# Attention keys moved between partitions by SP's transfers in place of ScalarE copies, in a two-layer hybrid decoder

## What is computed

```python
aq = apply_partial_rope(aq.reshape(B, S, nh, ATT_HEAD_DIM), cos, sin)
ak = apply_partial_rope(ak.reshape(B, S, nh, ATT_HEAD_DIM), cos, sin)
for gi, (window, dilation) in enumerate(ATT_GROUPS):      # (128, 1), (512, 4), (2048, 16)
    o, lse = dilated_window_attention(aq[:, :, hs], ak[:, :, hs], av[:, :, hs], window, dilation)
```

## Time and profile before

| | |
|---|---|
| runs, median (lowest to highest) | 1271.35 us (1270.79 to 1271.76) |
| profiled execution, span from first to last instruction | 1269.9 us; it has no other time of its own, so what lies around the span is taken as median less span, 1.45 us |
| granted TensorE clock, mean | 0.997 of full |
| PE busy | 1257.0 us, 99% |
| DVE / ACT / POOL busy | 893.0 (70%) / 705.4 (56%) / 244.0 us (19%) |
| bytes moved by DMA | 264.97 MB, mean 209 GB/s |

### The profile page before, as it was taken

One profiled execution on the slowest core, in us unless ns is written; L12 is line 12 of the kernel. 1 busy time (PEld: TensorE's weight loads), 2 busy tenths in 40 slices (PEclk: granted clock), 3 DMA queues, 4 the chain that ended last, 5 costly groups with the idle time before them and its releaser, 6 DMA issues.

```text
span 1269.9 us, 16388 instructions
## 1 busy us (share of the span) xinstructions
PE 1257.0 (99%) x6342; PEld 1040.2 (82%) x6342; DVE 893.0 (70%) x1229; ACT 705.4 (56%) x989; POOL 244.0 (19%) x268
## 2 busy tenths in 40 slices
PE   9999999999999999999999999999999999999996
PEld 8888888878888888888888788888888888888885
DVE  5686876876667655865785779768665776567656
ACT  5477476575555544444563775666755555345441
POOL 0321522522220000400003223334131200004000
PEclk9999999999999999999999999999999999999998
DMA  9968768765665555465657587678546556565562
GB/s 336 310 209 261 236 189 277 260 192 164 204 195 174 184 186 185 152 230 190 207 186 238 183 282 245 193 258 282 184 149 215 183 157 209 165 197 198 186 212 86
DMA packets 129277, 264.97 MB, mean 209 GB/s; under 512 B 8824, under 2 KB 8976, under 8 KB 128688
## 3 DMA queue, kind: packets, MB, share of 16 engines
q1 hardware_dynamic: 123712, 247.23, 60.6%
q0 software_dynamic: 3680, 13.28, 3.0%
q10 hardware_dynamic: 1808, 3.42, 0.7%
HBM read 258.61 MB, written 5.28 MB: 208 GB/s over the span
## 4 chain that ended last, share of the span: by engine, by line
PE 86%; ACT 4%; DVE 4%; POOL 3%; issue 2%; DVEq 0%; POOLq 0%; ACTq 0%
PE ps L373 79%; ACT arena L810 2%; DVE w_lo L1060 2%; ACT w_hi L736 2%; PE ps L444 1%; PE ps L671 1%; PE ps L391 1%; PE ps L639 1%; POOL arena L1684 1%; PE ps L533 0%; POOL arena L1680 0%; PE ps L518 0%; ACT arena L807 0%; PE ps L355 0%; DVE arena L1133 0%
## 5 line engine op out<-in xcount | busy, mean ns | idle before, releaser
L1060 DVE TENSOR_TENSOR w_lo<-w_raw,w_hi 128x1024 fp32r<-128x1024 f32 x408 | 527.1, 1305 | 326.4 <-ACT w_hi L736 324.5
L736 ACT ACTIVATE w_hi<-w_raw 128x1024 fp32r<-128x1024 f32 x408 | 427.3, 1058 | 388.9 <-PE ps L373 339.3
L373 PE MATMUL ps<-w_hi,xT_hi 128*128 128x512 f32 x1616 | 636.2, 394 | 0.7 <-DVE w_lo L1060 0.7
L373 PE MATMUL ps<-w_hi,xT_lo 128*128 128x512 f32 x1616 | 629.6, 390 | 0.0
L373 PE MATMUL ps<-w_lo,xT_hi 128*128 128x512 f32 x1616 | 629.0, 389 | 0.0
L373 PEld LDWEIGHTS ps<-w_hi,xT_hi 128*128 128x128 f32 x1616 | 303.4, 188 | 64.3 <-issue 1.3
L373 PEld LDWEIGHTS ps<-w_hi,xT_lo 128*128 128x128 f32 x1616 | 303.3, 188 | 64.0
L373 PEld LDWEIGHTS ps<-w_lo,xT_hi 128*128 128x128 f32 x1616 | 303.6, 188 | 61.4
L292 POOL TENSOR_TENSOR carried<-ident 1x1 f32<-1x1 f32 x30 | 19.6, 652 | 454.8 <-DVE arena L1416 178.7
L1217 DVE CUSTOM_DVE_ANT_0 mix<-xres,mix 128x1024 f32<-128x1024 f32 x64 | 89.0, 1390 | 1.1
L807 ACT ACTIVATE arena<-arena 32x256 f32<-32x256 f32 x128 | 53.2, 416 | 15.6 <-DVE arena L1137 14.0
(11 more groups left out here) (244 smaller groups left out, 825.3 us busy)
## 6 DMA issues: line engine op xcount, KB each, us to landing
w_raw<-w_in_dram SPq DMA_DIRECT2D x367, 512.0 KB, 4.5
w_raw<-w_out_dram SPq DMA_DIRECT2D x64, 512.0 KB, 4.8
mix<-gate_w_dram SPq DMA_DIRECT2D x32, 512.0 KB, 5.6
xres<-x_dram ACTq DMA_DIRECT2D x4, 512.0 KB, 8.4
v_dram<-arena POOLq DMA_DIRECT2D x4, 512.0 KB, 6.3
z<-v_dram POOLq DMA_DIRECT2D x8, 256.0 KB, 5.6
z<-ln_g_dram POOLq DMA_DIRECT2D x2, 1024.0 KB, 7.7
store<-ln_b_dram POOLq DMA_DIRECT2D x2, 1024.0 KB, 7.9
```

The costliest lines, as they stand in the source:

```text
L373: mm = pe.matmul(ps[2 * s + t][:], a[:, order[c] * KC + k, t * P:(t + 1) * P], b[:, k], start=(c + k + i == 0), stop=(c == CH - 1 and k == ...
L736: A(hi_of(n, c), w_raw[:, c % RING], ACT.Copy).then_inc(w_hi_done, 1)
L1060: TTn(lo_of(n, c), w_raw[:, c % RING], hi_of(n, c).bitcast(F32), ALU.subtract).then_inc(w_lo_done, 1)
```

## The change

Keys no longer go through ACT. After `turned`, SP issues sixteen transfers within SBUF (32 partitions x 256 elements, 32 KB each) from `zT[1]` to `kT`, in its queue after the load of piece 3 of block `n0+3` and behind a wait for the turn. A transfer keeps the order of elements in a partition (in comp groups two runs of 128 elements a partition, in group 2 one of 256), so `kT` now holds its columns in the order (u, t, m, ...) and PE reads them in runs of 8 elements (comp groups) or 32 (group 2). For that the key turn of group 2 writes its output in four strips. PE waits for `qT_act` (from ACT) and for 256 counts of `kT_landed`. ACT's `moved` handles queries alone.

```diff
--- before.py
+++ after.py
@@ -36,6 +36,7 @@
 ORDER = (1, 2, 0)
 NCOMP = 2
 RES = 4
+QUARTER = P // 4
 LEN = SEQ // RES
 SLOTS = TT * PAIRS
 QUADRANTS = ((0, 0), (1, 0), (0, 1), (1, 1))
@@ -110,13 +111,15 @@
             pass
         arena = sb("arena", [P, 8192])
         qT = arena[:, 0:1024].rearrange("p (m t) -> p m t", m=PAIRS)
-        kT = arena[:, 1024:2048].rearrange("p (m t) -> p m t", m=PAIRS)
+        kT = arena[:, 1024:2048]
         vA = arena[:, 2048:3072].rearrange("p (t c) -> p t c", t=TT)
         pr = arena[:, 3072:4608].rearrange("p (b h s) -> p b h s", b=2, h=2)
         pT_a = arena[:, 4608:5376].rearrange("p (h s) -> p h s", h=2)
         og = arena[:, 5376:6400].rearrange("p (t c) -> p t c", t=TT)
         oacc = arena[:, 6400:7424].rearrange("p (t c) -> p t c", t=TT)
-        qTr, kTr = (m.rearrange("p m (r i) -> p m r i", r=RES) for m in (qT, kT))
+        qTr = qT.rearrange("p m (r i) -> p m r i", r=RES)
+        kTr = kT.rearrange("p (u t m r i) -> p m r t u i", u=4, t=TT, m=PAIRS, r=RES)
+        kTt = kT.rearrange("p (u t m s) -> p m t u s", u=4, t=TT, m=PAIRS)
         vS = vA.rearrange("p t (h q d) -> p t q h d", h=2, q=PAIRS)
         prC = arena[:, 3072:4096].rearrange("p (s h i) -> p s h i", s=SLOTS, h=2)
         zp = arena[:, 0:1024]
@@ -216,7 +219,7 @@
         consts, tables = sem("consts"), sem("tables")
         own_dve, own_pool, own_act = sem("own_dve"), sem("own_pool"), sem("own_act")
         mask_set, roped, turned = sem("mask_set"), sem("roped"), sem("turned")
-        qk_ps, qkT_act, qkT_dve = sem("qk_ps"), sem("qkT_act"), sem("qkT_dve")
+        qT_act, kT_landed = sem("qT_act"), sem("kT_landed")
         scored, masked, probs = sem("scored"), sem("masked"), sem("probs")
         pT_ps, pT_act, pT_dve = sem("pT_ps"), sem("pT_act"), sem("pT_dve")
         pv_done, og_act, og_dve = sem("pv_done"), sem("og_act"), sem("og_dve")
@@ -298,6 +301,20 @@
         @block.sync
         def _(sp):
             for l in range(DEPTH):
+                def move_keys(g):
+
+                    sp.wait_ge(turned, l * (GROUPS * 2) + g * 2 + 2)
+                    for u in range(4):
+                        for f in range(4):
+                            dst = kT[f * QUARTER:(f + 1) * QUARTER, u * 256:(u + 1) * 256]
+                            src = zT[1][u * QUARTER:(u + 1) * QUARTER]
+                            if g < NCOMP:
+                                dst = dst.rearrange("p (t x) -> p t x", t=TT)
+                                src = src.rearrange("p (t f x) -> p f t x", t=TT, f=4)[:, f]
+                            else:
+                                src = src[:, f * 256:(f + 1) * 256]
+                            sp.dma_start(dst, src).then_inc(kT_landed, 16)
+
                 def load(w, n, col, order, gate=()):
 
                     for c in range(CH):
@@ -325,6 +342,8 @@
                                      w[l, rows:rows + KC * P, col:col + BW]
                                      .rearrange("(k p) n -> p k n", p=P)
                                      ).then_inc(w_landed[c % RING], 16)
+                        if c == 3 and N_LOOP < n < N_SU and (n - N_LOOP) % 4 == 3:
+                            move_keys((n - N_LOOP) // 4)
 
                 plain = tuple(range(CH))
                 load(w_in, 0, AG * BW, plain)
@@ -497,14 +516,15 @@
                     def scores(p):
 
                         if p == 0:
-                            pe.wait_ge(qkT_act, qk + 2)
+                            pe.wait_ge(qT_act, l * GROUPS + g + 1)
+                            pe.wait_ge(kT_landed, (l * GROUPS + g + 1) * 16 * 16)
                             pe.wait_ge(comp_og_act, comp)
                             pe.wait_ge(comp_og_dve, comp)
                         for h in range(2):
                             rows = slice(HD * h, HD * (h + 1))
                             o = ps[4 + 2 * (p % 2) + h]
-                            pe.matmul(o[:, 0:P], qT[rows, p, 0:P], kT[rows, p, 0:P], start=True, stop=True)
-                            mm = pe.matmul(o[:, P:3 * P], qT[rows, p, P:2 * P], kT[rows, p, :],
+                            pe.matmul(o[:, 0:P], qT[rows, p, 0:P], kTt[rows, p, 0], start=True, stop=True)
+                            mm = pe.matmul(o[:, P:3 * P], qT[rows, p, P:2 * P], kTt[rows, p],
                                            start=True, stop=True)
                         mm.then_inc(scored, 1)
 
@@ -537,14 +557,15 @@
 
                     def comp_scores():
 
-                        pe.wait_ge(qkT_act, qk + 2)
+                        pe.wait_ge(qT_act, l * GROUPS + g + 1)
+                        pe.wait_ge(kT_landed, (l * GROUPS + g + 1) * 16 * 16)
                         for j in range(TT):
                             for p in range(PAIRS):
                                 at = (j * PAIRS + p) * LEN
                                 for h, c in QUADRANTS:
                                     rows, r = slice(HD * h, HD * (h + 1)), 2 * j + c
                                     mm = pe.matmul(ps[4 + h][c * LEN:(c + 1) * LEN, at:at + LEN], qTr[rows, p, r, :],
-                                                   kTr[rows, p, r, :], start=True, stop=True)
+                                                   kTr[rows, p, r], start=True, stop=True)
                         mm.then_inc(comp_scored, 1)
 
                     def comp_values(comp):
@@ -795,13 +816,13 @@
                             src = src.rearrange("p (q h d) -> p q h d", q=PAIRS, h=2)
                         A(dst, src, ACT.Copy).then_inc(z_act, 1)
 
-                    def moved(which, first, last):
-
-                        act.wait_ge(turned, qk + which + 1)
+                    def moved(first, last):
+
+                        act.wait_ge(turned, qk + 1)
                         for i in range(first, last):
                             u, f = i // 4, i % 4
-                            src = zT[which][u * 32:(u + 1) * 32]
-                            dst = (qT, kT)[which][f * 32:(f + 1) * 32]
+                            src = zT[0][u * 32:(u + 1) * 32]
+                            dst = qT[f * 32:(f + 1) * 32]
                             if g < NCOMP:
 
                                 mv_ = A(dst.rearrange("p m (r t u i) -> p u t (m r) i", r=RES, t=TT, u=4)[:, u],
@@ -810,7 +831,7 @@
                                 mv_ = A(dst.rearrange("p m (t u s) -> p u t m s", t=TT, u=4)[:, u],
                                         src.rearrange("p (t m f s) -> p f t m s", t=TT, m=PAIRS, f=4)[:, f], ACT.Copy)
                         if last == 16:
-                            mv_.then_inc(qkT_act, 1)
+                            mv_.then_inc(qT_act, 1)
 
                     def comp_exponentials():
                         act.wait_ge(comp_masked, comp + 1)
@@ -869,14 +890,10 @@
                     split(n0 + 1, 4, 8)
                     for i in range(4):
                         split(n0 + 2, i, i + 1)
-                        moved(0, 4 * i, 4 * i + 4)
+                        moved(4 * i, 4 * i + 4)
                     take(n0 + 2, 0, z[:, 1, 0, :])
                     split(n0 + 2, 4, 8)
-                    split(n0 + 3, 0, 1)
-                    moved(1, 0, 8)
-                    split(n0 + 3, 1, 2)
-                    moved(1, 8, 16)
-                    split(n0 + 3, 2, 3)
+                    split(n0 + 3, 0, 3)
                     if g < NCOMP:
                         take(n0 + 3, 1, vS[:, 0])
                         split(n0 + 3, 3, 6)
@@ -1130,7 +1147,8 @@
 
                         dve.wait_ge(roped, qk + which + 1)
                         if g == NCOMP:
-                            V.transpose(zT[which], z[:, which].rearrange("p t c -> p (t c)")).then_inc(turned, 1)
+                            into = zT[which].rearrange("p (f b s) -> p b f s", f=4, b=TT * PAIRS) if which else zT[which]
+                            V.transpose(into, z[:, which].rearrange("p t c -> p (t c)")).then_inc(turned, 1)
                             return
                         for t in range(TT):
```

## The result

The kernel with the keys on SP takes 1305.9 us (median of 4 runs, 1304.27 to 1306.46); the kernel before, beside it, 1271.55 (4 runs, 1270.79 to 1272.06). The ratio is 1.0268, with a 95% interval of 1.0253 to 1.0283: **slower by 2.7%**, where the prediction said 1271.7 and at most 1277.5. The profiled execution has a span of 1302.5 us, 32.6 above the 1269.9 of before.

The account below looks back on a forecast made before the run. PE was taken to bound the kernel, a matmul stream without holes. Two group 2 stalls, 0.2 + 0.2 = +0.4 us, on span 1269.9 plus 1.45 to the median gave 1271.7 us; range 1270.6 to 1277.5.

Parts of the forecast that it names:

- What bounds the kernel: PE: busy 1257.0 of 1269.9 us, a matmul stream without holes; waits for ACT's copies only half a microsecond.
- Part 2, the pace: Sixteen key transfers on SP, one issued every 0.45 us, ends 0.38 and 0.64; +0.2 us in each layer's group 2.
- the corner at that end: Start-up pace of 0.64 us on SP: +12.6 us, all four comp groups stalling too; left out of the range.
- the slow landing: Rival: key transfers land after 2.7 us, about +3.0, 1274.4; 1278 with pace 0.54; chance 0.08 of exceeding 2.5 us.
- Part 2, the landing: Key transfers' time from issue to landing: 1.4 us, ends 1.2 and 2.7; keys ready at turn + 8.2 us.
- Part 1: ACT's 96 key copies removed, 39.9 us of ACT: at most -0.5 us; nobody on PE awaits the earlier hi pieces.
- Part 3: Weight loads queued behind SP's sixteen issues: zero, with 0.66 us cover in group 0 of layer 1.
- Part 4: Small ones: transfer traffic, one more PE wait, group 2's key turn in strips, PE's broken-up key reads; all taken zero.
- SP issues slowly in a burst: Rival: SP's key transfers at a pace of 0.54 us, total +3.9, 1275.3 us; chance 0.24.
- the turn and the reads: Rivals: group 2's key turn adds 0.86 a stall, 1273.4; PE reads keys twice as long, 1276.4, chance 0.05.
- What would show it: Signs: right, 16 SP issues some 7 us long; wrong, start-to-start 0.5 us or more, PE waiting 2 us in group 2.

Follow-up runs that it names:

- the idle transfers: Kernel before, ACT's copies kept, plus sixteen SP transfers a group into scratch that nobody on PE waits for: 1290.73 us; cut to 2 KB each, 1292.53 us.
- The version on two queues: Changed kernel with eight of a group's sixteen key transfers issued by SP and eight by ACT's own queue: 1270.75 us, ratio 0.9995.
- later scores: Changed kernel with PE taking the first scores one weight chunk later, behind three chunks in groups 0 and 1, two in group 2: 1295.57 us.

## Why the prediction was wrong

**What bounds the kernel** was read rightly: PE had no holes, and every microsecond that it waits for keys is on the path. So was the shape of the answer: nothing to gain but 0.5 us, everything to lose at six deadlines.

**Part 2, the pace, is the step that failed.** The term was mis-sized: taken at 0.45 us, it is 0.64. The reason given for the low value, "little is described by each", bears on nothing, since 2 KB and 32 KB are issued at one pace. The rows it rested on were loads from DRAM, which are of the other kind (0.46 in a burst); none of the rows of before is of the form SBUF to SBUF, and a pair was taken for a burst although the rival itself said that every longer burst in the trace spoke against it. That the high end was 0.64 to two digits is luck: it came from two issues of the start-up that are loads from DRAM too, a form that takes 0.44 to 0.51 in the bursts. Fifteen intervals multiply such an error: 0.19 x 15 is 2.9 us a group. Worse, the range left out the corner at that end, "+12.6 us", though the text itself names it; and its top of 1277.5 doesn't take in the burst pace with the slow landing, which the rival puts at 1278. Without v's store and loads the stalls come to about that corner: the four comp stalls of the kernel that holds them back (1.25, 1.12, 2.75, 1.09) make 13.0 us with group 2's two of the kernel after (3.14, 3.68), and 13.5 with its own two (3.41, 3.92). Pace and landing thus account for some 13 of the 32.6 us, store and loads for 10, the clock for 9.5.

**Part 2, the landing**, taken at 1.4 us, is 1.9 undisturbed, inside its range. The deadlines, 10.5, 9.4 and 7.5 us behind the turn, were right: from the turn's end at 88.66 the keys of group 0 should stand ready at 0.03 + 15 x 0.64 + 1.9 = 11.5 us, 1.0 past the deadline, and 1.25 was measured with store and loads held back. The Trainium skill ("SBUF — State Buffer", section The DMA setup-cost knee) gives every transfer a roughly fixed 2 us; the trace agrees with it, 1.9 for 32 KB and 1.8 for 2 KB, and not with my 1.4, reached from a 4 KB store to DRAM. For that form the trace stays below the page: 32 KB from SBUF to DRAM (L352) landed after 1.5 to 1.6 us. Of 96 landings the longest took 4.2 us, beside POOL's loads of v, beyond my high end of 2.7.

**Part 1 was wrong in "nobody on PE is waiting for" ACT's earlier work.** ACT's freed time let POOL's store of v go 5.5 us earlier, and its two loads of v behind it, onto the end of the key burst. That costs some 10 us in the four comp groups. I looked for what becomes late when work is added, not for what becomes early when it is removed.

**Part 3 took zero, with a cover of 0.66 us that holds "to a pace of 0.486"**; at 0.64 it doesn't. The rule was right for the comp groups and its input wrong. In group 2 it looked at `w_lo` alone, "not before 286", and missed ACT's exponentials, which stand behind the w_hi piece 4 and made PE wait 1.5 and 2.4 us with the idle transfers. In the changed kernel the loss doesn't show (0.7 us at `w_lo`, as before), since the wait for the keys is longer; the idle transfers show it bare, 19 us, and moving the deadline uncovers it.

**Part 4**: strips, broken-up reads, the extra wait: zero, as taken. The key turn in group 2 takes 1.23 us as in the earlier trace rows (278.19 1.23), `comp_scores` 1.16 as in the earlier trace rows. Traffic: zero for the key transfers on the loads (2 KB against 32 KB), but not for POOL's store and loads of v on the key transfers, which weren't considered.

**Missing altogether** was that a stall has a second price: the granted clock falls behind it, 9.5 us in all, 41% on top of the 23.1 us of stalls.

**The rivals.** "SP issues slowly in a burst" was the right mechanism with a chance of 0.24, but priced at 0.54 and not at 0.64. The landing added 0.5 us a stall by itself, the turn and the reads nothing. "What would show it" named the rows that then appeared: a start-to-start over 0.5, PE waiting for DMA into arena.

**A better kernel?** The version on two queues is the best of this family, 1270.75 us, and can't be told from before: PE had nothing more to give. One transfer for the four pieces of a quarter, which would cut the number of issues, wasn't tried.

## What to carry to other kernels

A burst of small transfers is priced by its number, not by its bytes: count the issues and take the interval from a burst of the same pair of memories. If there is none, keep the slowest adjacent pair in the range and say that its form is another. Then look at both sides of the issuing queue: what waits for the last transfer, and what stands behind it; the longer wait hides the other, and mending one uncovers it. On a path that PE bounds, add to a stall of some microseconds what the slower clock behind it costs, and ask what the relieved engine will start earlier and what that runs into.

## What the runs showed of the hardware

- SP issued small transfers between like memories (SBUF to SBUF, DRAM to DRAM) every 0.63 to 0.64 us in bursts, and 32 KB ones between unlike memories every 0.46. From SBUF to SBUF it was the same for 2 KB and 32 KB, and for 32 and 128 partitions. ACT's queue had 0.62 to 0.66 for the key transfers, beside SP's. The Trainium skill ("DMA: Bandwidth & Descriptors", section Issuing engines are not separate DMA queues) says that initiating on several engines saves only the sequencer's time, which is usually small beside the transfer. The mechanism fits; here the sequencer's time is what counts: sixteen issues last 10.3 us, a landing 1.9, and the split took 1305.9 us to 1270.75.
- Beside a 512 KB store of POOL's queue one SP issue of the burst took 1.21 us in place of 0.60, and landings took 2.6 to 3.0 us in place of 1.9; beside the two 256 KB loads behind it the last landings took 3.75 to 4.2. Held back, neither was seen.
- The first transfers of a burst, right behind a weight load, landed after up to 3.6 us (group 2 of layer 0), the last after 1.8.
- After all nine of PE's waits for keys of 2.7 to 5.2 us (the kernel after and the one with store and loads held back) its granted clock fell to the lower level, for 3.4 us and once 6.8, and after none under 1.8 us. In between the runs don't give a rule: of 14 waits of 1.88 to 2.5 us in the kernels with idle transfers and with later scores, six were followed by such a stretch, and the longest, 2.5, was not. Filling the stall with extra matmuls kept the clock up and made the kernel 6.9 us faster.
